# The first modulation in a new order of loads and projection pieces, and twelve scalings of x moved to GpSimd

## What is computed

```python
mod = jax.nn.silu(c) @ w_mod[l] + b_mod[l]                  # c_ctx for the prompt's tokens
shift, scale, gate = jnp.split(mod, 3, axis=-1)
xn = rmsnorm(x, norm_w) * (1.0 + scale[:, None, :]) + shift[:, None, :]
proj = xn @ w_in
```

## Time and profile before

| | |
|---|---|
| median of three runs | 2151.84 us (2149.92 to 2151.88) |
| the profiled execution, its own time | 2152.64 us |
| its span in the trace | 2150.8 us |
| PE matmul busy | 2106.6 us, 98% |
| DVE busy | 1442.9 us, 67% |
| ACT busy | 647.9 us, 30% |
| POOL busy | 194.0 us, 9% |
| DMA, mean over the span | 170 GB/s |
| granted clock of PE, mean | 0.997 |

### The profile page before, as it was taken

The page is one execution under the profiler, slowest core; times in us unless marked ns, Lnnn a source line. Parts: engine busy times, 40 slices in busy tenths (PEclk is TensorE's granted clock), DMA queues, the critical chain, the costliest instruction groups (busy, mean ns, idle before and its releaser), DMA issues.

```text
span 2150.8 us, 35018 instructions
## 1 busy us (share of the span) xinstructions
PE 2106.6 (98%) x13815; PEld 1895.5 (88%) x13815; DVE 1442.9 (67%) x2797; ACT 647.9 (30%) x1092; POOL 194.0 (9%) x125
## 2 busy tenths in 40 slices
PE   5999999999999999999999999999999999999998
PEld 3778887887999999999998888888899999999998
DVE  5869888999665656766366355466666566676644
ACT  4232221321333334442134212232133333343302
POOL 0000000000000000523221000000000000043331
PEclk9999999999999999999999999999999999999999
DMA  9989786774333324564435546445343233366443
GB/s 351 376 293 320 230 282 230 234 245 160 117 105 101 99 77 135 187 210 144 121 120 162 170 149 203 132 139 150 120 129 104 75 97 105 90 209 208 152 123 141
DMA packets 357333, 365.42 MB, mean 170 GB/s; under 512 B 17670, under 2 KB 264156, under 8 KB 356572
## 3 DMA queue, kind: packets, MB, share of 16 engines
q1 hardware_dynamic: 328528, 320.67, 46.6%
q10 hardware_dynamic: 28684, 43.09, 5.3%
HBM read 304.98 MB, written 58.72 MB: 169 GB/s over the span
## 4 chain that ended last, share of the span: by engine, by line
PE 70%; DVE 2%; issue 1%; ACT 1%; DMA 1%; SPq 0%; ACTq 0%; DVEq 0%
PE psP L921 20%; PE psP L865 16%; PE psP L942 10%; PE psO L1148 6%; PE psT L875 4%; PE psT L1148 3%; PE psO L1121 3%; PE psP L1076 3%; PE psT L1087 2%; PE psP L1160 0%; PE psP L1238 0%; DVE xf L2025 0%; PE psP L1246 0%; PE psP L834 0%; DMA old<-x_scratch 0%
## 5 line engine op out<-in xcount | busy, mean ns | idle before, releaser
L1831 DVE SCALAR_TENSOR_TENSOR macc<-mraw,cond,macc 128x384 f32<-128x384 f32 (+1 forms) x960 | 389.2, 477 | 0.0
L865 PE MATMUL psP<-x_high,high 128*128 128x512 f32 x864 | 342.3, 396 | 0.6 <-DVE x_low L1887 0.6
L865 PE MATMUL psP<-x_high,low 128*128 128x512 f32 x864 | 336.6, 390 | 0.0
L865 PE MATMUL psP<-x_low,high 128*128 128x512 f32 x864 | 336.4, 389 | 0.0
L1336 ACT ACTIVATE high<-raw 128x1024 fp32r<-128x1024 f32 x128 | 135.4, 1059 | 594.3 <-PE psT L875 493.3
L921 PE MATMUL psP<-x_high,high 128*128 128x320 f32 x1024 | 242.6, 318 | 0.0
L921 PE MATMUL psP<-x_high,low 128*128 128x320 f32 x1024 | 233.4, 309 | 0.0
L921 PE MATMUL psP<-x_low,high 128*128 128x320 f32 x1024 | 232.9, 309 | 0.0
L1849 DVE TENSOR_TENSOR low<-raw,high 128x1024 fp32r<-128x1024 f32 x128 | 163.3, 1277 | 64.8 <-ACT high L1336 64.7
L865 PEld LDWEIGHTS psP<-x_high,high 128*128 128x128 f32 x864 | 162.1, 188 | 41.6 <-issue 7.7
L865 PEld LDWEIGHTS psP<-x_high,low 128*128 128x128 f32 x864 | 162.2, 188 | 34.5
(11 more groups left out here) (327 smaller groups left out, 3715.5 us busy)
## 6 DMA issues: line engine op xcount, KB each, us to landing
raw<-in_w_in_dram SPq DMA_DIRECT2D x132, 512.0 KB, 6.0
wmod<-in_w_mod_dram SPq DMA_DIRECT2D x32, 1024.0 KB, 8.2
mraw<-in_w_mod_dram SPq DMA_DIRECT2D x64, 512.0 KB, 4.5
mraw<-in_w_mod_dram SPq DMA_DIRECT2D x32, 1024.0 KB, 7.3
raw<-in_w_in_dram SPq DMA_DIRECT2D x32, 1024.0 KB, 5.7
raw<-in_w_out_dram SPq DMA_DIRECT2D x64, 512.0 KB, 4.2
old<-x_scratch SPq DMA_DIRECT2D x64, 320.0 KB, 3.2
xf<-proj_scratch SPq DMA_DIRECT2D x48, 320.0 KB, 3.6
```

Source lines behind the costliest of these rows:

```text
L865: mm = pe.matmul(latent_ps[m], own, moved, start=(k == 0 and w is whole and x is x_high), stop=(k == KT - 1 and w is rest))
L1831: m = dve.scalar_tensor_tensor(acc[:, v, 0:width], mraw[hf][:, k, 0:width], c, acc[:, v, 0:width], ALU.mult, ALU.add)
```

## The change

- SP: chunks 0 and 1 are loaded in one go, and raw chunks 0 and 1 and the extra tiles behind them. From stage 1 on, the even raw chunk moves from between the two modulation chunks to the middle of the odd one.
- PE: the quarters of chunk 0 stand behind the transposes of tiles 3, 6, 8 and 11 (before 3, 7, 11 and 15). Two pieces of stage 0 go ahead of the first quarter of chunk 2 (`PIECES_LEAD`), and the pieces among chunks 2 and 3 are dealt out by `PIECES_FIRST`.
- ACT: the cast of raw chunk 1 moves from ahead of stage 0's four tiles to behind the first two.
- DVE: the low part of the even raw chunk moves from ahead of the early sums to behind `mod_sum`. DVE scales only the four tiles of stage 0.
- POOL: scales the other twelve tiles in one row, once DVE's four are done.

```diff
--- before.py
+++ after.py
@@ -95,7 +95,10 @@
 EXTRA_T, EXTRA_PIECES = 2, 4
 BLOCK_PIECES = BLOCK_C * PIECES + EXTRA_PIECES
 PIECES_AFTER, PIECES_LAST = [0, 2, 1, 2, 1, 2, 1, 2], 3
+FIRST_QUARTERS = (3, 6, 8, 11)
+PIECES_LEAD, PIECES_FIRST = 2, [0, 1, 1, 1, 1, 2, 1, 2]
 assert sum(PIECES_AFTER) + PIECES_LAST == BLOCK_PIECES and len(PIECES_AFTER) == 8
+assert PIECES_LEAD + sum(PIECES_FIRST) + PIECES_LAST == BLOCK_PIECES and len(PIECES_FIRST) == 8
 EXTRA_SLOT = RING - 1
 SUMMED_Q = 2
 EARLY0 = (BLOCKS - 1) * SUMMED_Q * BLOCK_K
@@ -476,9 +479,9 @@
 
             wm = io["w_mod"][0].rearrange("(k p) n -> p k n", p=P)
 
-            def mod_block(t):
-
-                for q in range(4):
+            def mod_block(t, quarters):
+
+                for q in quarters:
                     sp.wait_ge(s[f"wmod_used{q}"], t + SEED)
                     sp.dma_start(wmod[q][:], wm[:, q * KT // 4:(q + 1) * KT // 4, mod_at(t) * P:mod_at(t) * P + MOD_N])\
                         .then_inc(s[f"wmod_in{q}"], 16)
@@ -504,11 +507,17 @@
                              [:, j * BLOCK_K:(j + 1) * BLOCK_K, FRONT[1][0] * P:(FRONT[1][0] + EXTRA_T) * P])\
                     .then_inc(s[f"chunk_in{EXTRA_SLOT}"], 16)
 
-            for t in range(MOD_CHUNKS):
-                mod_block(t)
-                front_chunk(0, t)
-                if t % 2 == 1:
-                    extra_tiles(t // 2)
+            for j in range(BLOCKS):
+                mod_block(2 * j, range(4))
+                if j == 0:
+                    mod_block(2 * j + 1, range(4))
+                    front_chunk(0, BLOCK_C * j)
+                else:
+                    mod_block(2 * j + 1, range(SUMMED_Q))
+                    front_chunk(0, BLOCK_C * j)
+                    mod_block(2 * j + 1, range(SUMMED_Q, 4))
+                front_chunk(0, BLOCK_C * j + 1)
+                extra_tiles(j)
 
             def mod_weights(l, h):
 
@@ -806,8 +815,8 @@
                 for i in range(TT):
                     mm = pe.transpose(psP[k % 2][:, i * P:(i + 1) * P], xtok[:, i, k * P:(k + 1) * P], ident[:])
                 mm.then_inc(s["embed_turned"], 1)
-                if k % 4 == 3:
-                    mod_quarter(0, k // 4)
+                if k in FIRST_QUARTERS:
+                    mod_quarter(0, FIRST_QUARTERS.index(k))
             pe.wait_ge(s["x_squared"], 2 * TT)
             pe.matmul(rs_ps[0], ones[:], r_a[:, 0:DEC], start=True, stop=True)
             pe.matmul(rs_ps[1], ones[:], r_a[:, DEC:TOK], start=True, stop=True).then_inc(s["stat_summed"], 1)
@@ -1012,10 +1021,13 @@
 
                     pe.wait_ge(s["x_taken"], KT)
                     piece = 0
+                    for _ in range(PIECES_LEAD):
+                        block_piece(piece)
+                        piece += 1
                     for t in range(2, MOD_CHUNKS):
                         for q in range(4):
                             mod_quarter(t, q)
-                            for _ in range(PIECES_AFTER[t % 2 * 4 + q]):
+                            for _ in range((PIECES_FIRST if t < 4 else PIECES_AFTER)[t % 2 * 4 + q]):
                                 block_piece(piece)
                                 piece += 1
                         if t % 2 == 1:
@@ -1415,10 +1427,13 @@
 
                 if l == 0:
                     for j in range(BLOCKS):
-                        for n in (2 * j, 2 * j + 1):
-                            cast_chunk(n)
+                        cast_chunk(BLOCK_C * j)
+                        if j > 0:
+                            cast_chunk(BLOCK_C * j + 1)
                         act.wait_ge(s["mod_ready"], j + 1)
                         for k in range(j * BLOCK_K, (j + 1) * BLOCK_K):
+                            if k == BLOCK_K // 2:
+                                cast_chunk(BLOCK_C * j + 1)
                             slot = k % 2
                             act.wait_ge(s[f"scaled{slot}"], k // 2 + 1)
                             if k >= 2:
@@ -1888,9 +1903,9 @@
                                       ALU.subtract).then_inc(s["x_split"], 1)
 
                 if l == 0:
-                    def scale_block(j):
-
-                        for k in range(j * BLOCK_K, (j + 1) * BLOCK_K):
+                    def scale_first():
+
+                        for k in range(BLOCK_K):
                             dve.tensor_tensor(x_hat[:, k, :], xf[:, k, :], rstd[:], ALU.mult).then_inc(s[f"scaled{k % 2}"], 1)
 
                     def early_sums(t):
@@ -1925,18 +1940,17 @@
                         return mod_turn[t % 2].rearrange("p (j c) -> p j c", c=FLIP)[:, :, 0:2]
 
                     dve.wait_ge(s["head_ready"], 2 + DEPTH)
-                    scale_block(0)
+                    scale_first()
                     for j in range(BLOCKS):
                         if j > 0:
                             flip(2 * j)
-                        chunk_low(BLOCK_C * j)
-                        if j > 0:
                             early_sums(2 * j + 1)
                         flip(2 * j + 1)
                         dve.wait_ge(s["mod_turned"], 2 * j + 2)
                         mod_sum([(slice(j * BLOCK_K, (j + 1) * BLOCK_K), flipped(2 * j + 1)),
                                  (slice(KT + j * BLOCK_K, KT + (j + 1) * BLOCK_K), flipped(2 * j))],
                                 2 * j + 2, j * BLOCK_K, BLOCK_K)
+                        chunk_low(BLOCK_C * j)
                         for k in range(j * BLOCK_K, (j + 1) * BLOCK_K):
                             split_x(k % 2, k // 2)
                             if k % BLOCK_K == 1:
@@ -1944,8 +1958,6 @@
                         dve.wait_ge(s["chunk_cast"], extra_turn(j) + 1)
                         dve.tensor_tensor(extra_slot(low), extra_slot(raw), extra_slot(high).bitcast(F32), ALU.subtract)\
                             .then_inc(s["chunk_split"], 1)
-                        if j + 1 < BLOCKS:
-                            scale_block(j + 1)
                 else:
                     for slot in range(2):
                         split_x(slot, 0)
@@ -2318,6 +2330,10 @@
         def _(pool):
             for name in SEEDED:
                 pool.sem_inc(s[name], SEED)
+            for slot in range(2):
+                pool.wait_ge(s[f"scaled{slot}"], BLOCK_K // 2)
+            for k in range(BLOCK_K, KT):
+                pool.tensor_tensor(x_hat[:, k, :], xf[:, k, :], rstd[:], ALU.mult).then_inc(s[f"scaled{k % 2}"], 1)
             for l in range(DEPTH):
                 if l > 0:
                     arrive(pool)
```

## The result

| | before | after |
|---|---|---|
| median of eight runs | 2151.86 us (2149.92 to 2153.07) | 2157.70 us (2155.95 to 2159.74) |
| ratio to before | | 1.0026, 95% interval 1.0017 to 1.0035 |
| the profiled execution, its own time | 2152.64 us | 2159.74 us |

I go through the views in the order of the prediction. The totals say only that nothing big moved; they answer to the earlier trace rows.

The account below looks back on a forecast made before the run. PE, busy 98% of the span, was taken as the bound, so only its waits count: +9.5 us at the strip sums and -2.2 later made +7.3, 2159.1 us for the median; range 2150.8 to 2163.2.

Parts of the forecast that it names:

- mod_a ready: Stage 0, DVE: two additions to mod and mod_a wait for POOL products, moving it from 45.05 to 48.9 us.
- k = 1 split: Stage 0, DVE: the split x that PE's projection pieces need is finished at 59.4 us, against 49.49 before.
- nine matmuls at the low clock: Lead pieces ahead of chunk 2: PE's remaining matmuls take some 4.0 us at 1.2 GHz, ending at 63.4.
- DVE free: Stage 0: remaining products lengthen four more DVE instructions; the extra tiles' low part then ends the list at 69.8 us.
- turn of chunk 2: First modulation: PE's pieces and quarters set its start at 70.7 us, 11.0 later, just after DVE is free.
- strip sums: After chunk 2's turn: PE's strip sums start 10.31 us behind the early sums' start, at 81.4 against 71.84, +9.5.
- stages 2 and 3: Next two stages: moving the even raw chunk's low part removes nearly all PE's remaining waits for early sums, -2.2 us.
- sum: Whole kernel: +9.5 and -2.2 give +7.3 us, 2159.9 for an execution like the profiled one, 2159.1 for the median.
- The mechanism: Stage 0: POOL's products and DVE's instructions alternate, each product costing a DVE instruction 1.37 or 1.29 us.
- The blocked instructions: DVE's chain from chunk 1's turn up to k = 1: all eight instructions wait for a POOL product.
- The startup: Before DVE's four scalings end: an earlier quarter of chunk 0 adds a hole in DVE's copies, 0.85 us later.
- The later gain: Two stages after the strip sums: PE's remaining waits for early sums nearly vanish, -2.2 us.

Follow-up runs that it names:

- run with memsets: The change with DVE scaling all tiles and GpSimd first writing zeros into the twelve tiles where its products stood: 2148.43 us, ratio 0.9981.
- four products: The change with GpSimd scaling only stage 1's four tiles early and DVE scaling those of stages 2 and 3: 2153.05 us, ratio 1.0003.

## Why the prediction came out right, step by step

| step | predicted | measured in the change |
|---|---|---|
| DVE's four scalings end | 44.1 | 43.62 |
| turn of chunk 1 | 44.25 | 43.58 |
| mod_a ready | 48.9 | 46.83 |
| low part of raw chunk 0 ends | 51.5 | 47.96 |
| k = 1 split | 59.4 | 55.61 |
| nine matmuls at the low clock | 4.0 | 3.65 (55.66 to 59.31) |
| DVE free | 69.8 | 68.31 |
| turn of chunk 2 | 70.7, by PE | 68.24, by DVE |
| strip sums | 81.4 (+9.5) | 78.73 (+6.9) |
| stages 2 and 3 | -2.2 | -0.7 |
| sum | +7.3 | +5.8 in the medians, +7.1 in the profiled executions |

**The mechanism** held. The products and DVE's instructions alternate, the row starts just ahead of the chain that PE waits for, and PE stands until k = 1 is split, at 1.2 GHz (0.50) when the pieces come. The Trainium skill has the rule in "SBUF — State Buffer", section "Who interferes with whom": a DVE instruction with two SBUF inputs contends with a GpSimd instruction that reads SBUF and not with one that only writes it. The run with memsets agrees: 0.83 for a difference beside them, 2.04 beside products. That rule is about two inputs; the casts, with one, were lengthened beside both. A whole product as price would be 1.53 here; 1.26 and 1.18 were measured, since DVE's instruction loses only the rest of a product that started before it: `mod_a` starts 0.18 behind its product and ends 0.03 behind it.

**The blocked instructions** were too many by two. I let every one of eight up to k = 1 wait; the second addition and the first low part did not (1.47 for both additions, 1.21 for the low part). Each of these two starts 0.01 us ahead of a product (45.25 and 46.75 against 45.26 and 46.76). That is 1.4 us at mod_a and 1.4 at the low part, most of the 3.1 by which the chain from the turn on was shorter (12.03 us instead of 15.15). But the products that these two let pass were met by later instructions: the last x_low and the last low part, which I had free at 0.83 and 1.22, took 2.06 and 2.57. So the end of the list moved by only 1.5, from 69.8 to 68.3. The number of products sets the end of the list; which instruction meets which product sets only k = 1.

**The startup** was mis-sized: the extra hole in DVE's copies cost 0.35 and not 0.85, because two of the others shrank, from 1.45 to 1.13 and from 0.85 to 0.60.

**The turn of chunk 2** I had bound by PE, with DVE free 0.9 earlier. With k = 1 split 3.8 earlier, PE's fourth quarter ended at 66.39, about where the durations that I had used put it (66.8), and DVE's list came last. From the turn to the strip sums it took 10.5, as predicted (10.7).

**The later gain** of 2.2 is the term that failed. The waits it was made of did vanish, and alone the moved low part is worth 2.8. But in the change PE had just paused for 1.05 and 2.00 us, and the clock fell again. With the 1.7 us missing there some 0.5 is left of the 2.2; 0.7 was measured (6.9 at the strip sums, 6.2 where ScalarE takes the first finished part of the projection, 156.73 against 150.57). Other runs fit a fall after a pause: with pauses of 0.93 and 0.34 (four products) and of 1.79 (DVE scaling) the clock stays at 1.00 there; after one of 2.33 (the products in DVE's pauses) it is 0.71 and 0.50 in the next two stretches. No run changed the pause alone. The two errors, 2.6 too much at the strip sums and 1.5 too little behind them, took each other partly away, and that is luck. So is the near match of +7.3 with the profiled executions' +7.1: 6.2 of it is there at 157 us, the rest comes later, in no term of the sum, and the change's profiled execution is the slowest of its eight.

That loads stopped from 56 to 60 us fits SP's list, where chunk 3's quarters wait for slots that PE frees late. What it cost stays open: the wait of 1.05 behind it is not longer than the 1.79 without the row.

The best kernels measured are the change with DVE scaling, with the even raw chunk in either place: ratio 0.9979, 4.5 us below the kernel before and some 10 below the change; the runs with memsets (0.9981) and with the products in DVE's pauses (0.9984) can't be told from them.

## What to carry to other kernels

Work that is moved to GpSimd is not free beside DVE, even when GpSimd has nothing else to do: count the products that stand in a row beside DVE's list, multiply by what one costs DVE (1.2 to 1.3 us here for 128x640 in float32, from 0.83 to 2.04 in the rows), and ask whether that list is awaited. Start such a row where DVE waits for another engine, or leave the work on DVE when PE waits for neither. A gain that is a wait removed must be asked again after the change has made new pauses: here the clock fell behind them, and most of the gain was gone.

## What was not expected of the hardware

- Beside GpSimd's memsets (0.66 us each), DVE's casts took 0.71 to 0.79 instead of 0.49, while differences and low parts kept their times.
- In these rows whoever starts first runs through, by however little. Taken one by one, the second addition (45.25) and the first low part (46.75) start 0.01 us ahead of a product and keep their 0.15 and 1.21. In the run with the row alone both additions take 0.56: they start at 44.95, when their product has only until 45.41 to go.
- GpSimd's product grew from 1.53 to 1.96 us in the row while DVE's instructions grew by 1.1 to 1.4: neither engine wins, they take turns.
